# A hybrid block and two DeepNorm layers on one core: head loop rearranged, masked scores, norm taken out of the operand, modulation by pairs of tiles

## What is computed

```python
u = rmsnorm(h, norm_mix); proj = u @ w_in               # u_ssm, q, k, v
y_ssm = s5_branch(u_ssm, ...)                           # diagonal complex recurrence, GELU, GLU
y_attn = stick_breaking_attention(q, k, v)              # 8 heads of 64
g_ssm, g_attn = split(sigmoid(u @ w_gate + b_gate))
h = h + (g_ssm * (y_ssm @ w_up_ssm) + g_attn * (y_attn @ w_up_attn)) @ w_out
hid = relu(rmsnorm(h, norm_mlp) @ w_ff1); h = h + (hid * hid) @ w_ff2
x = rmsnorm(h, norm_final)
for l in range(2):                                      # hybrid_layer
    shift, scale, gate = split(silu(c) @ w_ada[l] + b_ada[l])
    u = x * (1 + scale) + shift                         # then w_in, convolutions, latent attention, merge, w_o
    x = layer_norm(ALPHA * x + gate * out, ln_g, ln_b)
```

## Time and profile before

| | us |
|---|---|
| median of 3 runs | 1154.83 (1153.38 to 1159.17) |
| the profiled execution, its own time | 1156.74 |
| its span, first to last instruction | 1155.0 |
| TensorE busy | 1051.6 (91%) |
| VectorE busy | 719.8 (62%) |
| ScalarE busy | 539.5 (47%) |
| GpSimd busy | 355.1 (31%) |
| mean granted clock of TensorE | 0.947 of full |

### The profile page before, as it was taken

The page is one execution under the profiler, slowest core; times in us unless marked ns, Lnnn a source line. Parts: engine busy times, 40 slices in busy tenths (PEclk is TensorE's granted clock), DMA queues, the critical chain, the costliest instruction groups (busy, mean ns, idle before and its releaser), DMA issues.

```text
span 1155.0 us, 19572 instructions
## 1 busy us (share of the span) xinstructions
PE 1051.6 (91%) x8104; PEld 984.3 (85%) x8104; DVE 719.8 (62%) x1076; ACT 539.5 (47%) x620; POOL 355.1 (31%) x151
## 2 busy tenths in 40 slices
PE   4989999778799999987999989998799999899985
PEld 3977767568699999977999989998689999899984
DVE  4938887536432522335877896656448778977553
ACT  5443554533254444426554644543355546445433
POOL 3087772000178787820136600000001356000000
PEclk8977999899999999998999999999999999899988
DMA  8542443456545565545453455464454543544601
GB/s 256 183 146 74 146 141 127 135 181 205 189 155 183 157 202 189 170 155 186 147 178 116 146 161 167 134 199 163 125 184 147 182 130 133 168 154 147 217 3 37
DMA packets 159497, 179.57 MB, mean 155 GB/s; under 512 B 5041, under 2 KB 141745, under 8 KB 159409
## 3 DMA queue, kind: packets, MB, share of 16 engines
q1 hardware_dynamic: 159024, 177.22, 47.5%
q0 software_dynamic: 384, 1.10, 0.3%
HBM read 177.26 MB, written 1.05 MB: 154 GB/s over the span
## 4 chain that ended last, share of the span: by engine, by line
PE 74%; DVE 11%; issue 6%; ACT 5%; POOL 3%; DMA 1%; SPq 0%; ACTq 0%; DVEq 0%; POOLq 0%
PE pg L1643 22%; PE pg L1644 21%; PE pg L1645 21%; DVE area L1144 2%; DVE w_lo L1135 1%; ACT w_hi L852 1%; PE p_s L1733 1%; PE p_y L1799 1%; ACT area L830 1%; DVE area L1152 1%; PE p_o L1833 1%; PE p_s L1637 1%; DMA raw<-in_w_in 1%; DVE rows L1180 1%; ACT h L830 1%
## 5 line engine op out<-in xcount | busy, mean ns | idle before, releaser
L1643 PE MATMUL pg<-u_hi,w_hi 128*128 128x256 f32 x1664 | 488.7, 294 | 42.7 <-DVE u_lo L1144 38.3
L1644 PE MATMUL pg<-u_lo,w_hi 128*128 128x256 f32 x1664 | 479.8, 288 | 0.0
L1645 PE MATMUL pg<-u_hi,w_lo 128*128 128x256 f32 x1664 | 479.3, 288 | 0.0
L1643 PEld LDWEIGHTS pg<-u_hi,w_hi 128*128 128x128 f32 x1664 | 328.3, 197 | 51.4 <-issue 46.5
L754 POOL TENSOR_TENSOR w_lo<-raw,w_hi 128x2048 fp32r<-128x2048 f32 x58 | 268.2, 4634 | 301.5 <-ACT w_hi L852 301.5
L1644 PEld LDWEIGHTS pg<-u_lo,w_hi 128*128 128x128 f32 x1664 | 328.8, 198 | 0.7
L1645 PEld LDWEIGHTS pg<-u_hi,w_lo 128*128 128x128 f32 x1664 | 328.6, 197 | 0.0
L852 ACT ACTIVATE w_hi<-raw 128x2048 fp32r<-128x2048 f32 (+3 forms) x153 | 274.9, 1803 | 73.8 <-issue 38.6
L1135 DVE TENSOR_TENSOR w_lo<-raw,w_hi 128x2048 fp32r<-128x2048 f32 (+3 forms) x95 | 201.3, 2129 | 82.8 <-ACT w_hi L852 82.6
L858 ACT ACTIVATE area<-pg 128x512 f32<-128x512 f32 (+1 forms) x92 | 54.1, 588 | 170.3 <-PE pg L1645 158.5
L1643 PE MATMUL pg<-vb_hi,w_hi 128*128 128x256 f32 x320 | 93.8, 293 | 12.9 <-DVE area L1162 6.9
(11 more groups left out here) (203 smaller groups left out, 1326.6 us busy)
## 6 DMA issues: line engine op xcount, KB each, us to landing
raw<-in_w_in SPq DMA_DIRECT2D x68, 1024.0 KB, 5.2
raw<-in_w_ff SPq DMA_DIRECT2D x32, 1024.0 KB, 5.6
raw<-in_w_ada SPq DMA_DIRECT2D x24, 1024.0 KB, 5.2
raw<-in_w_gate SPq DMA_DIRECT2D x8, 1024.0 KB, 7.7
raw<-in_w_o SPq DMA_DIRECT2D x8, 1024.0 KB, 5.3
raw<-in_w_out SPq DMA_DIRECT2D x4, 1024.0 KB, 6.6
raw<-in_w_b_out SPq DMA_DIRECT2D x4, 1024.0 KB, 5.0
raw<-in_w_c_out SPq DMA_DIRECT2D x4, 1024.0 KB, 5.1
```

The source lines that it names most:

```text
L1643: pe.matmul(dst, w_h, x_h, start=first, stop=False)
L1644: pe.matmul(dst, w_h, x_l, start=False, stop=False)
L1645: return pe.matmul(dst, w_l, x_h, start=False, stop=last_)
```

## The change

Four parts. (a) The head loop: gate panel 0 goes ahead of the loop, gate panel m+1 stands in head m behind the next `ada` panel, `s5_out` moves ahead of it, `gate_ahead` looks one panel further, the loop has 8 turns instead of 9, and the GELU is made once for all four tiles behind the loop. `table` waits for each pair of states by itself. (b) Scores are masked first (`stick_scores` on VectorE adds the mask into `stick_z`, two buffers; log1p is made in the bank `p_z`), the mask product goes, `stick_fails` no longer repeats the q-k products, and `stick_weights` adds the masked scores and clips with a Relu. (c) The norm before `ff1`: `u2` is h * gain without 1/rms, made piece by piece as the pieces of `w_out` are added; 1/rms is multiplied in as the `ff1` results are taken. Two `ada` panels move behind `ff1` 0 and 1. (d) The later norms: h * 1/rms by pairs of tiles (`scaled`), gain and shift on ScalarE into `tmp`, then rounded from there; `prescale` is eight scaled copies. In the first panel on a new operand both column blocks now use a piece of `u` before the next piece is waited for (`blocks`). GpSimd makes one mask fewer.

```diff
@@ -139,9 +139,7 @@
         step("ada_take", i + 1)
         ada_panel(i + 2)
         step("ada_turn", i + 1)
-        if k == 2:
-            step("modulate", 0)
-        step("split", key)
+        step("modulate", key[1])
         step("ada_take", i + 2)
 
 
@@ -165,50 +163,47 @@
     step("table", 1)
     step("bu", 0)
     step("stick_scores", 0)
+    panel("gate", 0, 0, "w_gate", 0, 0, KT, 256, 1)
     ada_panel(0)
     step("ada_take", 0)
-    for m in range(HEADS + 1):
+    for m in range(HEADS):
         f = m // 2
         if m:
             step("stick_weights", m - 1)
-        if m < HEADS:
-            step("stick_soft", m)
-            step("state", 2 * m)
-            step("gate_ahead", len(panels))
-            step("stick_fails", m)
+        step("stick_soft", m)
+        if m % 2 and f:
+            step("s5_y", f - 1)
+        step("state", 2 * m)
+        if m + 1 < HEADS:
+            step("gate_ahead", len(panels) + 1)
+        step("stick_fails", m)
         step("ada_turn", m)
         if m + 1 < HEADS:
             step("stick_scores", m + 1)
-        if m < HEADS:
-            step("bu", 2 * m + 1)
+        step("bu", 2 * m + 1)
+        if m:
+            step("s5_out", m - 1)
+        ada_panel(m + 1)
+        step("ada_take", m + 1)
         if 2 * m + 2 < PAIRS:
             step("bu", 2 * m + 2)
-        if m % 2 and f:
-            step("s5_y", f - 1)
-        if m % 2 == 0 and f >= 2:
-            step("s5_gelu", f - 2)
-        if m < HEADS:
-            panel("gate", 0, m, "w_gate", 0, 256 * m, KT, 256, 1)
-        if m:
-            step("s5_out", m - 1)
-        if m == HEADS:
-            step("s5_y", WT - 1)
-            step("s5_inner", WT - 1)
-        if m < HEADS:
-            step("state", 2 * m + 1)
-        if m % 2 and f:
-            step("s5_inner", f - 1)
+        if m + 1 < HEADS:
+            panel("gate", 0, m + 1, "w_gate", 0, 256 * (m + 1), KT, 256, 1)
+        else:
+            step("stick_weights", m)
+        step("state", 2 * m + 1)
         if m in (2, 4):
             step("table", f + 1)
         if m:
             step("stick_out", m - 1)
-        if m < HEADS:
-            ada_panel(m + 1)
-            step("ada_take", m + 1)
+    step("stick_out", HEADS - 1)
+    step("ada_turn", HEADS)
+    step("s5_out", HEADS - 1)
+    step("s5_y", WT - 1)
     step("split", "ctx")
     ada_panel(9)
     step("ada_take", 9)
-    step("s5_gelu", WT - 1)
+    step("s5_gelu")
     step("split", "y")
     panel("up_attn", 0, 0, "w_up_attn", 0, 0, WT, 512, 2)
     step("ada_turn", 9)
@@ -237,13 +232,24 @@
             step("ada_end", 0)
         if n:
             norm_sums(1, n - 1)
-    norm_steps(1, "u2", 14)
+    step("split_ahead", count["split"] + 1)
+    step("u2_piece", 0)
+    ada_panel(14)
+    norm_sums(1, 3)
+    for j in range(1, 4):
+        step("u2_piece", j)
+    step("ada_take", 14)
+    step("norm", 1)
     chunks = DFF // W
     for c in range(chunks + 1):
         if c < chunks:
             for n in range(2):
                 panel("ff1", 0, 2 * c + n, "w_ff1", 0, W * c + 256 * n, KT, 256, 1)
-                if (c, n) == (0, 0):
+                if c == 0:
+                    step("ada_turn", 14 + n)
+                    ada_panel(15 + n)
+                    step("ada_take", 15 + n)
+                if (c, n) == (1, 0):
                     step("ada_turn", 16)
                     step("ada_end", 1)
         if c >= 1:
@@ -251,6 +257,7 @@
                 panel("ff2", 0, 2 * (c - 1) + n, "w_ff2", W * (c - 1), 512 * n, WT, 512, 2)
         if c == 2:
             step("rope_tables")
+            step("modulate_columns", 0)
     for j in range(3):
         norm_sums(2, j)
     norm_steps(2, ("u", 0), 17)
...
-                if f >= 2:
-                    pool.wait_ge(sem("state"), over("state", FOUR * (f - 2) + FOUR - 1))
                 for half in range(2):
+                    if f >= 2:
+                        pool.wait_ge(sem("state"), over("state", FOUR * (f - 2) + 2 * half + 1))
...
+            def u2_piece(j, _):
+
+                if j == 0:
+                    act.wait_ge(sem("groups"), OPERANDS["u2"]["after"] + 1)
+                for s, v in emptied([groups_of("out")[j]]):
+                    act.wait_ge(s, v)
+                for i in (2 * j, 2 * j + 1):
+                    fn(u_hi[:, i, :], h[:, i, :], ACT.Identity, scale=col("norm_mlp", i)).then_inc(*(c.event("hi", "u2", j) if i % 2 else c.step()))
+
+            def modulate(l, _):
+
+                o = OPERANDS["u", l]
+                act.wait_ge(sem("groups"), o["after"] + 1)
+                act.wait_ge(sem("scale1"), over("scale1", l))
+                for j in range(4):
+                    act.wait_ge(sem("ln_rows"), over("ln_rows", l - 1, j))
+                    for i in (2 * j, 2 * j + 1):
+                        fn(tmp[:, i, :], h[:, i, :], ACT.Identity, bias=shift1[:, i:i + 1],
+                           scale=scale1[:, i:i + 1]).then_inc(*c.step())
+                    fn(u_hi[:, 2 * j:2 * j + 2, :], tmp[:, 2 * j:2 * j + 2, :], ACT.Copy).then_inc(*c.event("hi", ("u", l), j))
 
...
+            def s5_gelu(_, __):
+                act.wait_ge(sem("y_rows"), over("y_rows", WT - 1))
+                fn(yt, yv, ACT.Square).then_inc(*c.event("y_sq"))
+                act.wait_ge(sem("y_inner"), over("y_inner"))
+                fn(yt, yt, ACT.Sigmoid, scale=2 * math.sqrt(2 / math.pi) * 0.044715).then_inc(*c.event("y_sig"))
 
             def stick_scores(hd, _):
 
-                act.wait_ge(sem("z"), over("z", hd))
                 if hd == 0:
                     act.preload_act_table_set("natural_log_exp_and_others")
-                else:
-
-                    act.wait_ge(sem("soft"), over("soft", hd - 1))
-                fn(stick[0], p_z[:, 0:384], ACT.Abs).then_inc(*c.step())
-                fn(stick[0], stick[0], ACT.Exp, scale=-1.0).then_inc(*c.step())
-                fn(stick[0], stick[0], ACT.Ln, bias=1.0).then_inc(*c.event("log1p", hd))
+                act.wait_ge(sem("masked"), over("masked", hd))
+                fn(p_z[:, 0:384], stick_z[hd % 2], ACT.Abs).then_inc(*c.step())
+                fn(p_z[:, 0:384], p_z[:, 0:384], ACT.Exp, scale=-1.0).then_inc(*c.step())
+                fn(p_z[:, 0:384], p_z[:, 0:384], ACT.Ln, bias=1.0).then_inc(*c.event("log1p", hd))
 
             def stick_weights(hd, _):
                 act.preload_act_table_set("natural_log_exp_and_others")
                 act.wait_ge(sem("logw"), over("logw", hd))
-                fn(stick[2 + hd % 2], stick[2 + hd % 2], ACT.Exp).then_inc(*c.event("w_stick", hd))
+                fn(stick_w[:, hd % 2], stick_w[:, hd % 2], ACT.Relu, scale=-1.0).then_inc(*c.step())
+                fn(stick_w[:, hd % 2], stick_w[:, hd % 2], ACT.Exp, scale=-1.0).then_inc(*c.event("w_stick", hd))
...
-                fn(h[:, :, :], h[:, :, :], ACT.Copy, scale=ALPHA).then_inc(*c.event("alpha_h", l))
+                for j in range(KT):
+                    fn(h[:, j, :], h[:, j, :], ACT.Identity, scale=rest_g[:, j:j + 1]).then_inc(*(c.event("alpha_h", l) if j == KT - 1 else c.step()))
...
+            def scaled(l):
+
+
                 before = c.last
-                for j in range(KT):
-
+                for j in range(4):
                     dve.wait_ge(*before)
-                    dst = tmp[:, j, :] if k < 2 else h[:, j, :]
-                    ins = dve.scalar_tensor_tensor(out=dst, in0=h[:, j, :], scalar=col(name, j), in1=rstd[:, 0, :],
-                                                   op0=ALU.mult, op1=ALU.mult)
-                    ins.then_inc(*(c.event("h_rows", j) if k == 2 else c.event("rows", key, j // 2) if j % 2 else c.step()))
-                    if k < 2 and j % 2 and j >= 3:
-                        low(key, j // 2 - 1)
-                if k < 2:
-                    low(key, 3)
+                    dve.tensor_tensor(h[:, 2 * j:2 * j + 2, :], h[:, 2 * j:2 * j + 2, :], spread(rstd[:, 0, :], P, 2, T),
+                                      ALU.mult).then_inc(*c.event("ln_rows", l, j))
+                    if j and l < LAYERS - 1:
+                        if j == 1:
+                            low_halves(first_splits(find("q_lat", l + 1, 0)["s"] + 1, ahead))
+                        low(("u", l + 1), j - 1)
+                if l < LAYERS - 1:
+                    low(("u", l + 1), 3)
+
+            def u2_piece(j, _):
+
+                dve.wait_ge(sem("hi"), over("hi", "u2", j))
+                for i in (2 * j, 2 * j + 1):
+                    stt(u_lo[:, i, :], h[:, i, :], col("norm_mlp", i), u_hi[:, i, :].bitcast(F32), ALU.mult,
+                        ALU.subtract).then_inc(*(c.event("lo", "u2", j) if i % 2 else c.step()))
...
+            def s5_gelu(_, __):
+
+                dve.wait_ge(sem("y_sq"), over("y_sq"))
+                stt(yt, yt, 1.0 / 0.044715, yv, ALU.add, ALU.mult).then_inc(*c.event("y_inner"))
+                dve.wait_ge(sem("y_sig"), over("y_sig"))
```

(50 more changed lines are left out.)

103 lines of the change are left out of this document (25 added, 78 removed).

## The result

The changed kernel takes 1142.46 us (median of 4 runs, 1140.59 to 1146.48) against 1157.0 for the kernel before on the same chip (1153.38 to 1159.48): ratio 0.9881, 95% interval 0.9839 to 0.9923. So it is faster by more than the 0.5% that can be told from no change, and 1138 was forecast, with 1123 to 1149 as the range. The profiled run of the changed kernel was the slowest of its four; its span is 1144.7 against 1155.0, so the two traces account for 10.3 of the 14.5 us.

The account below looks back on a forecast made before the run. TensorE, busy 91% of the span, was taken as the bound, so only its waits, needless work and low clock could be won. Terms summed to -16.9 from 1156.74, giving 1139.8 and a median of 1138; range 1123 to 1149.

Parts of the forecast that it names:

- loop start: Start of the head loop: one more gate panel done but no time won, 0.0; -6.6 if GpSimd were not late.
- steady heads: Four heads in mid-loop: 14.2 us each without repeated q-k products and GELU steps, -5.9 (bounds -8.7 to 0).
- loop end: Head 6's `stick_fails` to `up_attn`: 40.0 us instead of 43.54, -3.5; without the DMA wait 14.5 less.
- GELU tail: Behind the loop: GELU in one piece delays the splits and take queued behind it, +4.5 (bounds 0, +6).
- norm before `ff1`: Between `w_out` and `ff1`: pieces of `u2` no longer wait for the norm, -7.0 (bounds -2.5, -9.5).
- layer 0 with prescale: Norm before layer 0, -3.5 by the new chain of pieces, and `prescale` as eight operations, +1.4.
- layer 1: Norm before layer 1: the same chain as in layer 0 ends at 843.1 against 845.7, -2.6.
- The two new waits: TensorE waits 6 us before gate 2 for GpSimd's low half and 9 before `stick_fails` 7 for `up_attn` 0's DMA.
- rival 3: Head loop keeps its pace: 15.7 us a head gives 1144 (chance 0.1); 17 or more, 1149 and up (0.08).
- rival 2: Norm before `ff1`: GpSimd's low half holds VectorE, +4.3, giving 1142; chance 0.1.
- `up_attn` starts at F+40.0: Loop end: `up_attn` starts 40.0 us after head 6's `stick_fails` (F), against 43.54 before.
- the prescale's +1.4: Layer 0: `prescale` as eight operations takes 5.45 us instead of 1.9, costing +1.4 (bounds 0, +3.5).

Follow-up runs that it names:

- norm1_old: Changed kernel with the norm before `ff1` as in the kernel before: ratio 0.9929 to the kernel before, 5.3 us slower than the changed kernel.
- combined: Changed kernel with `table` 1 behind gate 2's low half, no early `up_attn` 0 split, GELU behind that panel, head 7's softmax weights ahead of `ada` 8: 1115.8 us, 0.9659.
- gelu_late: Changed kernel with GELU and the halves of y issued behind the `up_attn` 0 panel: 1138.58 us, ratio 0.987 to the kernel before.
- qk_again: Changed kernel with the two repeated q-k products of each head back in `stick_fails`: ratio 0.9937 to the kernel before, 6.2 us slower than the changed kernel.

## Why the prediction was right, point by point

| Term | forecast | in the two traces | by experiment |
|---|---|---|---|
| loop start | 0.0 | +0.2 | without GpSimd's delay -6.5 (forecast -6.6) |
| steady heads | -5.9 | -7.4 | q-k products 3.4 of it |
| loop end | -3.5 | -0.3 | without the DMA's wait 13.9 less (forecast 14.5) |
| GELU tail | +4.5 | +7.5 (4.6 up to `ada` 10) | GELU behind the panel: 1.5 less by ratio |
| norm before `ff1` | -7.0 | -7.0 up to `ff1` 2, -8.0 from `out` 0 to `ff1` 7 | -5.3 by ratio |
| layer 0 with prescale | -2.1 | -1.8 | both layers -7.0 by ratio |
| layer 1 | -2.6 | -0.2 | |
| sum (with -0.3 for blocks) | -16.9 | -10.3 at the end | -13.5 by ratio |

**Right.** The forecast's mechanisms are all there. The two new waits that it worked out from the order alone stand where it put them, with 5.2 for 6 and 9.02 for 9, and taking each away gave nearly what it had said: -6.5 for -6.6, 13.9 for 14.5. Head 2 starts at 118.33, forecast 118.2; `q_lat` of layer 0 starts 4.3 us behind the reciprocal, forecast 4. No wait stands before `ff1` 0 and 3.9 before `ff1` 1, forecast 3. TensorE paces the heads (rival 3 fell), and GpSimd is out of the way at the norm (rival 2 did not arise).

**Partly luck.** The sum was too large: -16.9 forecast, 13.5 measured by ratio. It would have been further off if errors had not offset each other: the steady heads gave 1.5 us more than forecast, the loop end gave 3.2 less. The range held the result because it was wide, and that 1142 is also rival 2's number says nothing for rival 2.

**Mis-sized: the loop end.** The step that ends in "`up_attn` starts at F+40.0" came out at F+43.25. Fails 7 (F+22.9) and the end of state 15 (F+34.9) came within 0.3 us of the forecast. From there the prediction went straight to `s5_out` 7; TensorE has `stick_out` 7 and the turn of `ada` 8 in front of it, and it began `s5_out` 7 only 2.67 us behind state 15. It left out a wait: ScalarE has the copy of `ada` 8 ahead of the softmax weights of head 7. ScalarE's timeline shows it:

```profile
206.62 0.38 ACT L861 ACTIVATE root<-pg 128x256 f32<-128x256 f32 x1 [9.59 <-PE pg L1696]
207.03 1.28 ACT L1046 ACT_TABLE_LOAD   x1
208.32 1.08 ACT L833 ACTIVATE area<-area 128x384 f32<-128x384 f32 x2
```

VectorE had the input of the weights ready at 203.15; the weights came at 209.4. That is the 2.02 before `stick_out` 7. How much it costs hangs on the clock too: eight traces with this same loop end and its wait gave 39.7 to 43.6 us, and in the shortest (`norm1_old`) `s5_out` 7 ran at full clock, 2.0 us instead of the 3.6 forecast and the 3.7 measured here. With the weights early and without the DMA's wait the loop end took 26.2 in `combined`, near the 25.5 that the prediction's own sum gives without the wait.

**Mis-sized: what a hole costs behind it.** The prediction counted low clock in and right behind its two holes in the loop, and none further on. After `ada` 10 the second `up_attn` panel took 0.142 us a matmul against 0.122, `glu` 0.174 against 0.153 and `up_ssm` 0.148 against 0.136, 3.1 us together, and the stretch from `ada` 10 to `out` 0 became 2.9 longer. In layer 1 the chain's gain was eaten likewise. The stretch of layer 1 in which the latent sums stand, first in the changed kernel, then in `gelu_late`:

```profile
846.09:852.71 6.62, 4.61 (x13) 3.14 (x13) 1.88 (x1) 6.26 (x11) 0.00 (x0) 0.74 0.31 92
```
```profile
838.12:843.06 4.94, 2.94 (x14) 2.01 (x13) 1.89 (x1) 4.67 (x8) 0.00 (x0) 1.00 0.43 124
```

The same work takes TensorE 4.61 us at a granted clock of 0.74, so partly at its 1.2 GHz level, and 2.94 at 1.00. Where the clock did not fall (`gelu_late`, `qk_again`), layer 1 gave 2.8 us, near the forecast 2.6. In layer 0 the norm itself gave 3.3 of the 3.5, and the prescale's +1.4 did not show: no wait stands there, and the 1.7 lost at that place are this low clock. The Trainium skill (TensorE: Matmul & The Clock Gate, HAM oscillation) says that bursts between waits start throttled again; the rows agree as to place, and not every such burst did so.

## What to carry to other kernels

An engine that works in order and looks ahead for the next weights can be stopped by a transfer that nobody needs yet: for every split or table that is issued early, work out when its input lands and what is queued behind it. Here two such places, both to be read from the order before the change was built, cost more than the change won: 6 to 8 and 9 to 11 us against 13.5. Price a hole on TensorE by its length and the slow matmuls behind it, and count on a part of any local gain being given back where the clock falls anew.
